# Order of the exponentials of pass A and of the value products in an attention stage

## What is computed

```python
# forgetting attention, 8 heads of 64: causal, with a bias of summed log forget gates
s = q @ k.T * HD ** -0.5 + c[:, None] - c[None, :]
s = where(kpos <= qpos, s, NEG_INF)
of = softmax(s) @ v
# difference attention, 4 heads, two maps of 64 each, value width 128
s_m = q_m @ k_m.T * HD ** -0.5 + bias[t5_bucket(kpos - qpos)]
s_m = where(kpos // 64 <= qpos // 64, s_m, NEG_INF)
od = (softmax(s_0) - lam * softmax(s_1)) @ v
```

## Time and profile before

| | |
|---|---|
| median of 3 executions | 2587.92 us |
| lowest, highest | 2584.03, 2592.81 us |
| the profiled execution's own time | 2590.08 us |
| its span, first to last instruction | 2588.3 us |
| mean granted TensorE clock | 0.985 of full |
| TensorE busy (matmul) | 2476.8 us, 96% |
| weight loads busy | 1975.2 us, 76% |
| VectorE busy | 1372.5 us, 53% |
| ScalarE busy | 943.0 us, 36% |
| GpSimd busy | 382.7 us, 15% |

### The profile page before, as it was taken

The page is one execution under the profiler, slowest core; times in us unless marked ns, Lnnn a source line. Parts: engine busy times, 40 slices in busy tenths (PEclk is TensorE's granted clock), DMA queues, the critical chain, the costliest instruction groups (busy, mean ns, idle before and its releaser), DMA issues.

```text
span 2588.3 us, 35100 instructions
## 1 busy us (share of the span) xinstructions
PE 2476.8 (96%) x13569; PEld 1975.2 (76%) x13569; DVE 1372.5 (53%) x2227; ACT 943.0 (36%) x1869; POOL 382.7 (15%) x398
## 2 busy tenths in 40 slices
PE   7999999999999999999999999899899989999998
PEld 5788888789999999999955565565565556888997
DVE  5311123314443333442368788788788886655553
ACT  4123331112222222111136646655664666322221
POOL 0100001122100000112352123103212242000000
PEclk9999999999999999999989999999999999999999
DMA  5688878948977666897660523235055123544432
GB/s 152 158 224 206 210 201 205 205 137 238 255 230 231 202 193 189 241 227 164 175 162 6 127 55 85 53 79 131 5 132 108 28 91 111 178 130 129 146 117 90
DMA packets 583893, 388.67 MB, mean 150 GB/s; under 512 B 318672, under 2 KB 538776, under 8 KB 577416
## 3 DMA queue, kind: packets, MB, share of 16 engines
q1 hardware_dynamic: 574592, 367.80, 54.1%
q0 software_dynamic: 9136, 18.63, 2.1%
HBM read 284.83 MB, written 134.79 MB: 162 GB/s over the span
## 4 chain that ended last, share of the span: by engine, by line
PE 78%; DVE 6%; ACT 5%; issue 4%; SPq 3%; DMA 3%; POOL 1%; DVEq 0%; ACTq 0%; POOLq 0%
PE p_acc L876 14%; PE p_acc L880 13%; PE p_acc L881 13%; PE a_op L2122 5%; PE a_sb L2097 4%; PE a_sb L2098 3%; PE a_op L2119 3%; PE a_sa L2072 2%; PE a_sa L2075 2%; PE e_U L1428 2%; PE e_U L1430 2%; PE e_U L1429 2%; ACT a_e L1931 2%; PE a_sa L2073 2%; DVE a_nmax L1962 2%
## 5 line engine op out<-in xcount | busy, mean ns | idle before, releaser
L876 PE MATMUL p_acc<-p_h_hi,p_w_hi 128*128 128x384 f32 (+1 forms) x1960 | 715.9, 365 | 7.9 <-DVE p_ev L586 5.2
L881 PE MATMUL p_acc<-p_h_hi,p_w_lo 128*128 128x384 f32 (+1 forms) x1920 | 687.5, 358 | 0.0
L880 PE MATMUL p_acc<-p_h_lo,p_w_hi 128*128 128x384 f32 (+1 forms) x1920 | 687.2, 358 | 0.0
L1962 DVE TENSOR_REDUCE a_nmax<-a_sa 128x1 f32<-128x1024 f32 (+7 forms) x384 | 346.9, 910 | 126.2 <-PE a_sa L2075 48.8
L1931 ACT ACTIVATE a_e<-a_sb 128x512 f32<-128x512 f32 (+3 forms) x640 | 310.5, 533 | 269.4 <-PE a_sb L2098 174.6
L876 PEld LDWEIGHTS p_acc<-p_h_hi,p_w_hi 128*128 128x128 f32 x1960 | 370.3, 189 | 48.8 <-issue 12.8
L881 PEld LDWEIGHTS p_acc<-p_h_hi,p_w_lo 128*128 128x128 f32 x1920 | 361.5, 188 | 30.6
L880 PEld LDWEIGHTS p_acc<-p_h_lo,p_w_hi 128*128 128x128 f32 x1920 | 361.8, 188 | 29.5
L692 DVE TENSOR_TENSOR p_w_lo<-p_raw,p_w_hi 128x1024 fp32r<-128x1024 f32 x96 | 130.3, 1357 | 357.9 <-ACT p_w_hi L619 357.8
L2097 PE MATMUL a_sb<-a_q,a_k 128*128 128x512 f32 (+2 forms) x640 | 276.9, 436 | 20.6 <-ACT a_e L1931 18.1
L2098 PE MATMUL a_sb<-a_q,a_k 68*128 68x512 f32 (+2 forms) x640 | 237.6, 374 | 0.0
(11 more groups left out here) (233 smaller groups left out, 3465.9 us busy)
## 6 DMA issues: line engine op xcount, KB each, us to landing
p_raw<-in_w_in SPq DMA_DIRECT2D x98, 512.0 KB, 5.6
s_k_raw<-scratch_kS SPq DMA_DIRECT2D x64, 512.0 KB, 6.9
scratch_kS<-in_cache_fox_k SPq DMA_DIRECT2D x32, 512.0 KB, 6.5
scratch_kS<-in_cache_diff_k SPq DMA_DIRECT2D x32, 512.0 KB, 6.4
s_v_raw<-in_cache_fox_v SPq DMA_DIRECT2D x8, 2048.0 KB, 10.8
s_v_raw<-in_cache_diff_v SPq DMA_DIRECT2D x8, 2048.0 KB, 10.1
a_q<-scratch_q_hi SPq DMA_DIRECT2D x32, 512.0 KB, 13.1
a_k<-scratch_k_hi SPq DMA_DIRECT2D x32, 512.0 KB, 18.2
```

The lines of the kernel that those rows point to most:

```text
L876: nc.tensor.matmul(acc[a % 2][:, 0:n], hi, h_hi[p][:, k, at:at + n], start=(k == 0), stop=False)
L880: nc.tensor.matmul(acc[a % 2][:, 0:n], hi, h_lo[p][:, k, at:at + n], start=False, stop=False)
L881: last = nc.tensor.matmul(acc[a % 2][:, 0:n], lo, h_hi[p][:, k, at:at + n], start=False, stop=(k == DK - 1))
L1962: nc.vector.tensor_reduce(nmax[:, b % 2, c, col:col + 1], scores_of(ev[1]), axes, ALU.max, negate=True).then_inc(a_maxed, 1)
```

## The change

Two edits, both in `events()`. First, a helper `ready_early(u)` is asked ahead of B.u and E.u in every step. It is true when the last pass A unit handed out belongs to a difference pair, is not the last of its block, has its X not yet in the list, and either u is a difference unit in the band or two value products have been appended behind that unit. Then X of that unit is put ahead of B.u and E.u, and not again behind the next A. Second, value products of forgetting pairs are appended four at a time, V.u-5 to V.u-2, in steps with u % 4 == 1 in place of two in each odd step. No instruction is added or taken away, no size or buffer changes; only places in the list do.

In the third round the list changes so: X.253, X.263, X.268 and X.270 come ahead of E.186, E.194, E.198 and E.200; X.272, X.273, X.274 ahead of E.201 to E.203; X.278 and X.280 to X.283 ahead of E.207 to E.211. Over all rounds 48 of the 192 exponentials of pass A move, 36 of them to steps in the band. The bursts of value products are 10 in a round instead of 20, in steps 165, 169, ... 201; the one in step 201 is V.196, V.197, V.198, SUM.19, V.199, where before V.196 and V.197 stood in step 199.

```diff
--- before.py
+++ after.py
@@ -1615,6 +1615,15 @@
         head[22] += [("LV", 0)]
         head[HEAD_FIRST] += [("I", 3)]
         out, finish = [], []
+        summed = set()
+
+        def ready_early(u):
+
+            a = done - 1
+            if not done or a in summed or not is_diff(A_UNITS[a][0]) or a == a_last[A_UNITS[a][0]]:
+                return False
+            behind = [ev_ for ev_ in out[out.index(("A", a)):] if ev_[0] == "V"] if ("A", a) in out else []
+            return in_band(*B_UNITS[u]) or len(behind) >= 2
 
         def close(to, step):
 
@@ -1642,7 +1651,7 @@
                     while any(step[0] == "F" and step[1] <= b - 2 for step in finish):
                         stages(1)
                 out.append(("A", done))
-                if done > a_first[b]:
+                if done > a_first[b] and done - 1 not in summed:
                     out.append(("X", done - 1))
                 if done == a_last[b]:
                     finish.extend(("X", done) if n == "X" else ("F", b, n) for n in FINISH)
@@ -1679,6 +1688,9 @@
                 out += [("L", f + 1, 0), ("L", f + 1, 1)]
             if u == ONES_AT:
                 out.append(("ONES",))
+            if ready_early(u):
+                out.append(("X", done - 1))
+                summed.add(done - 1)
             out += [("B", u), ("E", u)]
             if u >= 1:
                 out.append(("W", u - 1))
@@ -1690,9 +1702,9 @@
             stages(1)
             if u >= 2 and is_diff(B_UNITS[u - 2][0]):
                 multiply(u - 2)
-            elif u >= 3 and u % 2:
-                multiply(u - 3)
-                multiply(u - 2)
+            elif u >= 5 and u % 4 == 1 and not is_diff(B_UNITS[u - 2][0]):
+                for x in range(u - 5, u - 1):
+                    multiply(x)
             for _ in share:
                 stages(1)
             if b // BLOCKS == FT - 1:
```

## The result

| | before | after |
|---|---|---|
| median | 2588.64 us (4 runs) | 2619.14 us (4 runs) |
| lowest, highest | 2584.03, 2592.81 | 2612.19, 2623.23 |
| the profiled execution's own time | 2590.08 | 2612.19 |
| its span, mean granted clock | 2588.3, 0.985 | 2610.3, 0.979 |
| ratio of the times | | 1.0115, 95% interval 1.0084 to 1.0147 |

The change makes the kernel 30 us slower; 2582 was forecast, with a range to 2603. The profiled execution of after is the fastest of its four, so its trace shows 22 of the 30 us. What follows the attention stage is as before (the stage ends 407.4 us before the last instruction, 407.9 before the change). The stage before it is 3.6 us shorter (the attention starts at 1302.8 in place of 1306.4), with 3.4 us at 1.2 GHz in it in place of 10.2. So the attention stage itself is 26.1 us longer (900.1 in place of 874.0).

The account below looks back on a forecast made before the run. TensorE was taken as the bound where other work covers pass A's ring through VectorE and ScalarE. Per round -1.4 + 4.8 - 4.1 - 0.9 = -1.6, four rounds -6.4: 2590.08 to 2583.7, as median 2582, range 2564 to 2603.

Parts of the forecast that it names:

- The walk through the round: Attention stage, period by period between kept bursts, then the band: -1.4 + 4.8 - 4.1 - 0.9 = -1.6 us a round.
- the clock: Half-rate stretches in the attention stage: may move by one per round, +-6.4 us, counted in the range only.
- the opened ring: Pass A's score product, VectorE reduction, ScalarE exponential, next-but-one score product: TensorE waits where removed pairs stood, 181 to 197.
- Price of a burst: Going in and out of a burst of 64-column value products on TensorE costs 0.34 us.
- The holes at 181 to 197: Five periods of the forgetting pair: TensorE only partly moves up where pairs stood, +4.8 us a round (bounds -1.7, +8.6).
- The end of the pair: Last kept burst to SUM.19: waits go, VectorE's queue sets SUM at 10.1 us, -4.1 a round (bounds 0, -6.5).
- Exponentials in the band: Difference pair: first block 0, second block -0.9 us a round, as waits for X.278 and X.280 go (bounds 0, -1.3).
- The slower rival: Holes open, the pair's end gains nothing (+13.6 us), clock adds 6.4: 2610, about 2608 as median; chance 0.22.
- The rule against the change: Trainium skill: interleave regimes with different busiest engines; value products four at a time undo some interleaving, so slower.

Follow-up runs that it names:

- the mix: Exponentials moved, value products in fours only in the first two blocks of each forgetting pair and its last burst, against the kernel before: 2560.46 us, ratio 0.9901.

## Why the prediction was wrong

**The walk through the round held in the main, and the clock did not.** Periods of the third round, from the burst of one kept step to the next, in us:

| period to u | before | after | change | forecast | half rate in it |
|---|---|---|---|---|---|
| 169, 173, 177 | 29.94 | 29.40 | -0.54 | -1.0 | 0 |
| 181 | 13.27 | 16.46 | +3.2 | +1.1 | 6.8 |
| 185 | 12.52 | 13.91 | +1.4 | +1.3 | 0 |
| 189 | 11.86 | 16.80 | +4.9 | +1.4 | 6.8 |
| 193 | 14.53 | 14.67 | +0.1 | +0.1 | 0 |
| 197 | 12.18 | 15.80 | +3.6 | +0.9 | 6.8 |
| 201 | 15.44 | 11.35 | -4.1 | -4.1 | 0 (3.4 before) |

Together +8.6 against a forecast of -0.3. The half rate is worth up to 10.2 us after and 1.7 before; what remains is +0.1, beside the -0.3 forecast. Where no half rate lies the forecast stands within 0.1 us except in the first three (the period to 177 was +0.1, forecast -0.34), and where it lies the miss is 2.1 to 3.5 against the 3.4 that 6.8 us at half rate can cost.

**What half rate costs.** The rounds repeat the same instructions, and some of them ran at full clock. First the third and the fourth block of the kernel before, each in the third round (none at half rate) and in the second (3.4 us of it); then the period to 197 of after, in the second round (none) and in the third (6.8 us):

```profile
1780.91:1816.08 35.17, 31.05 (x143) 17.22 (x142) 29.78 (x45) 20.78 (x51) 12.27 (x13) 1.00 0.43 98
1561.19:1597.98 36.79, 32.66 (x143) 17.82 (x142) 29.79 (x45) 20.78 (x51) 13.85 (x16) 0.95 0.43 95
1816.08:1866.30 50.22, 45.92 (x199) 26.29 (x197) 40.12 (x53) 34.72 (x76) 12.29 (x16) 1.00 0.02 6
1597.98:1649.81 51.83, 47.50 (x199) 26.78 (x197) 40.12 (x53) 34.83 (x75) 10.69 (x13) 0.97 0.02 6
```

```profile
1635.24:1648.81 13.57, 11.64 (x50) 6.73 (x48) 9.91 (x11) 8.68 (x18) 2.21 (x2) 1.00 0.00 1
1857.74:1873.54 15.80, 14.35 (x50) 8.46 (x49) 10.00 (x11) 8.76 (x18) 1.74 (x2) 0.78 0.00 1
```

That is 1.6 us more for 3.4 at half rate, twice, and 2.2 for 6.8, so 0.33 to 0.47 for each microsecond. Of the 49 us that the third and fourth blocks grew, 26 to 37 are then the clock (an estimate, for the 79 us more at half rate in them) and 12 to 23 the opened ring. The clock also hid a small miss of the walk: at full clock the period to 197 is 1.4 us longer than before (12.18 to 13.57), where +0.9 was forecast.

Point by point:
- *Price of a burst* (0.34, and the earlier trace rows): right. The first two periods, with TensorE free to move up, went from 11.23 to 10.92 and from 8.71 to 8.38, so -0.31 and -0.33. The Trainium skill (TensorEngine Tiling (Array Packing), Key Properties) gives the drain as a rule without a price; the trace agrees, and it is small beside what the place of a burst is worth.
- *The holes at 181 to 197*: right in place (1.22 ahead of pass A, 1.37 and 1.43 for E at u = 189, 2.06 for X.260), and in size where the clock stayed.
- *The end of the pair*: right to 0.1 us, SUM 10.12 behind the burst where 10.1 was worked out. But this period held 3.4 us or more at half rate in each round before and none after, so up to 1.7 us of the 4.1 in the third round are the clock's, and the agreement is in part luck.
- *Exponentials in the band*: -0.9 forecast for the second difference block, measured 90.7 to 86.7 over the four, -1.0 each on the mean. For the first difference block 0 was forecast, and 65.9 went to 58.0. These blocks had 27 us at half rate before and none after, worth up to 13.6, so the runs do not show how much of the 7.9 is anything else. Nor did this gain last to the next kept burst: from the burst of step 201 to that of step 165 a round later it is 106.1 us before (1659.01 to 1765.08) and 106.3 after (1660.18 to 1766.51), where -0.9 and one of the -0.34 had been forecast.
- *The clock*: this step failed. I took half-rate stretches as noise that "may move by one per round, +-6.4" about a mean of no change, since the trace before shows one fourth block with a stretch and one without. But in the runs half-rate time goes with TensorE's own idle time in the rings (up with the holes, 41 to 92 us, and down to 51 when they are filled), and the same sum said that four more holes would open in each round. It should have been a term with a sign: half-rate time went to 14 to 37 us in a round, in the stage from 41 to 92 us, up to 25.6 us of loss, where the range allowed 6.4. Forecast -6.4 + 25.6 = +19 stands beside 22 of the profiled executions, but that is in part luck of what is counted: with the start of the stage it is 58 to 96 us, so at most -6.4 + 18.8 = +12, beside the 26.1 us that the stage grew. The missing 14 us are terms of the sum that were too low, as above, and are not split further.
- *The slower rival* had the holes and the clock as its sum of +20 (2608) and came closest, but its deciding point, an end of the pair that gains nothing, did not happen, and its clock term (6.4) was a quarter of what the half rate could cost here. It had the right sign by a partly wrong mechanism. The trace cannot show the 7 us more of the median over the profiled execution, but in the four executions of after the mean clock falls as the time rises (0.979, 0.978, 0.974, 0.972 at 2612.19, 2615.34, 2622.93, 2623.23): by 2 x span x (1 - clock) the slowest has 37 us more at half rate than the fastest, and is 11 us longer.
- *The rule against the change* (the Trainium skill, Perfetto Trace Analysis, Optimization Strategy: interleave regimes with different busiest engines): the runs agree. Bursts kept two at a time in the ring-bound blocks are worth 59 us between after and the mix (2619.14 to 2560.46).

How much of a microsecond at half rate is lost depends on what runs then. Before, 27 of its 41 us lay in the first difference block, where the earlier trace rows show no engine full; there 3.4 us more at half rate cost 0.5 us (15.9 us in the third round, 16.4 in the second). After, all of it lies in blocks where TensorE has bursts to do. So the forgetting blocks alone had 14 us at half rate before and 92 after, up to 39 us of loss, which the 51 us of difference over the stage understate. What stays open is the exact split between clock and waits: the third blocks of after never ran at full clock, so their price is carried over from other stretches. And what decides which stretch of idle time brings a fall was not tested.

## What to carry to other kernels

A block of work that an order places into another chain's waits is worth more than its own switching cost: joining it elsewhere saves 0.34 us and can open a hole of 1.2 to 2.1 us. Where TensorE is the bound, idle time that an edit opens on it can cost twice, once as a wait and once as work at half rate behind it, and here the second was the larger part; a cheap test is to fill the hole with useless matmuls and see if the kernel gets faster, with an eye on the filler's own waits. Where a kernel repeats its rounds, compare the same block at both clocks to read the price. Join bursts where TensorE has work without waits around them, leave them apart where a ring through other engines has to be covered, and try a reordering with and without its neighbour, since an exponential moved early only paid with a burst over its chain.

## What was not expected of the hardware

The clock fell to 1.2 GHz without any long wait: a stretch of 7.00 us with TensorE busy 5.06 and no wait over 0.82 us was followed by 6.8 us at half rate. The Trainium skill (TensorE: Matmul & The Clock Gate, A second HAM failure mode: psum-queue depth-cycling) tells of a kernel whose short idle times between groups of matmuls made the clock oscillate, and the trace agrees in kind: this ring through two PSUM buffers, in float32, has 16 falls of the clock in the third and fourth blocks of after, where the kernel before has 4. And 128 additional matmuls of 256 columns made a kernel 14 us faster (2619.14 to 2605.24), while in another place, four times with waits of their own, they made it 12 us slower.
